# Expert rows gathered as quarters and turned by VectorE's block transposes

## The chip, the cores and the metric

The kernel runs on one core of a Trainium2 chip. The metric is device time in microseconds, of one launch. The core has TensorE (PE: matmuls and their weight loads), VectorE (DVE), ScalarE (ACT), GpSimd (POOL, which also issues the indirect transfers here) and SyncE (SP, which issues the others), and 16 DMA engines that all transfers share.

## What is computed

A residual block for 2048 tokens of 1024 features in float32: a token mixer (gated linear attention and sliding-window attention), then a mixture of 32 experts with two experts a token, then a final norm. The change lies in the experts:

```python
def hier_moe(u, ...):                      # u = rms_norm(h) * norm2_w
    g_w, g_idx = top_k(softmax(hf @ w_group + b_group), 1)        # one group of 4
    e_val, e_idx = top_k(logits of the 8 experts of the group, 2)
    gate = softmax(e_val) * g_w
    # rows sorted by expert; for every expert e and its rows xb:
    y = (silu(xb @ w_gate[e]) * (xb @ w_up[e])) @ w_down[e]       # 1024 -> 512 -> 1024
    out[token] += gate * y
h = h + hier_moe(rms_norm(h, norm2_w)); y = rms_norm(h, final_norm_w)
```

## The kernel before

**Stages.** The mixer runs first, 128 tokens an iteration, some 935 us. It leaves the residual rows in HBM (scratch "h", the trace's h_dram) and the normalised rows, without the weight norm2, in scratch "v2" (v_dram). Routing follows (`routing`), until about 970 us: every token-expert pair gets a slot, and tables of indices are made. Then comes the loop over the 32 experts (`experts`), 971.7 to 1759.3 us, and a short end. An expert has 160 slots: 128 main rows and 32 in a "tail". What exceeds them goes to a path for overflow, which the functions named `..._over` hold and which has no work in these runs. By the number of its rows an expert is computed 128, 144 or 160 wide (`WIDTHS`, `by_width`).

**How the parts talk.** Each engine runs its own loop over the experts, and semaphores hold them together. `after(eng, "m_", name, n)` waits until n steps of `name` are done in all.

**One expert on TensorE** (`pe_chunk`): `pe_gate` (L1324), four groups of eight matmuls into G = banks 0 and 1; `pe_up` (L1337), the same into U = banks 2 and 3; `pe_x` for the next expert, steps 0 and 1: eight transposes (L1291) of the gathered rows by a matmul with the identity, into banks 4 and 5; the down product of the tail into bank 0 (L1351, not at width 128); the first half of the down product of the main rows into bank 6 (L1365); `pe_x` step 2, two transposes of the tail's quarters; at 144 and 160 the matmul L1372, which sums the tail's squares over its four quarters and waits for ScalarE's `m_tail_square`; the second half of the down product into bank 7. The next gate waits for the tail's sum, since both use bank 0.

**VectorE:** four products `hT` = U x silu(G) (L1433); `dve_x` for the next expert, which evacuates the transposed rows times norm2 into `xT` (L1409, L1414); `dve_tail` (L1441), which adds the tail's rows, held as quarters of 256 columns on four groups of 32 partitions, to `sums_quarters`, once the base rows have landed; `dve_sums` (L1449, two halves); `dve_scale` (L1457, L1458), which makes the output rows from the roots.

**ScalarE:** four SiLUs (L1379), the tail's squares (L1389), the main rows' squares (L1392).

**POOL** (an iteration e): `copy_index` (L1277) once the transposes of expert e+1 are done, `gather` for expert e+2, as one transfer of 128 rows of 4 KB (L1264) and one of 128 quarter rows of 1 KB for the tail (L1266), into `xg`; then `move`: the move indices (L1199), `put_sums` (L1212, L1214: the sums of expert e to h_dram), `roots` (L1220, L1222), and, when the put has landed, `gather_base` (L1204, L1206: base rows of expert e+1 from h_dram, to which its result is added), and `put_out` (L1227, L1229). The base rows can only be gathered after the sums of the last expert have landed, since a token has two experts. Before the loop the rows of experts 0 and 1 are gathered.

**SyncE:** w_gate, w_up and w_down of the next expert (2 MB each, L1189), each as soon as its last matmul of this one is done. There is one buffer of each.

## Time and profile before

| | us |
|---|---|
| median of three runs | 1778.04 (1775.43 to 1778.35) |
| the profiled execution, as a whole | 1777.08 |
| its span, first to last instruction | 1774.8 |
| TensorE busy in the span | 1710.6 (96%) |
| VectorE, ScalarE, POOL busy | 669.0, 503.7, 387.6 |
| first gate to the last expert's end on TensorE | 971.7 to 1759.3 |

All durations below come from the profiled execution. The time of an execution is its span and some 2 us around it. A busy TensorE is not a TensorE at its peak, since ends of matmuls are modelled: what a group of matmuls costs is read from start to start.

### The profile page before, as it was taken

How to read it: one execution, taken by the hardware profiler on the slowest of the kernel's cores; microseconds unless marked ns; L12 is line 12 of the kernel's file. 1: busy time of each engine (PE TensorE's matmuls, PEld its weight loads, DVE VectorE, ACT ScalarE, POOL GpSimd, SP SyncE). 2: the span in 40 equal slices, each digit the busy share in tenths (PEclk: the TensorE clock that was granted, in tenths of full speed). 3: DMA queues.
4: the chain of work that ended last, by engine and by line, in shares of the span. 5: the costliest groups of instructions: out<-in, count | busy, mean ns of one | idle time of the engine just before them, and what ended most of it. 6: DMA issues, size and time to landing. Idle time of an engine off the chain costs nothing. (4 is left out here: it accounts for less than half of the span.)

```text
span 1774.8 us, 31842 instructions
## 1 busy us (share of the span) xinstructions
PE 1710.6 (96%) x11222; PEld 1271.9 (72%) x11223; DVE 669.0 (38%) x1721; ACT 503.7 (28%) x1318; POOL 387.6 (22%) x522
## 2 busy tenths in 40 slices
PE   6899999999999999999968999999999999999996
PEld 5676675766757667676647788778878788878784
DVE  1344345543455434554357222222222222222222
ACT  1444424444244442444423111111111111111111
POOL 0001011010100101001011234334434344434333
PEclk9999999999999999999989999999999999999998
DMA  9521122211222112121124889889999999989994
GB/s 356 119 74 47 60 83 71 71 47 59 83 71 71 45 61 83 71 71 43 63 93 151 299 293 353 309 308 329 325 332 340 301 339 330 339 306 350 324 313 138
DMA packets 156873, 333.69 MB, mean 188 GB/s; under 512 B 23797, under 2 KB 43482, under 8 KB 156836
## 3 DMA queue, kind: packets, MB, share of 16 engines
q1 hardware_dynamic: 131204, 277.82, 46.0%
q0 software_dynamic: 24768, 55.26, 8.8%
q8 instruction: 25, 0.41, 0.1%
q10 hardware_dynamic: 864, 0.10, 0.0%
q14 instruction: 12, 0.10, 0.0%
HBM read 298.74 MB, written 63.70 MB: 204 GB/s over the span
## 5 line engine op out<-in xcount | busy, mean ns | idle before, releaser
L328 PE MATMUL bank<-uT,w_in_sb 128*128 128x128 f32 x2304 | 277.2, 279 | 2.3 <-DVE uT L676 2.3
L328 PEld LDWEIGHTS bank<-uT,w_in_sb 128*128 128x128 f32 x2304 | 268.3, 195 | 11.1 <-issue 8.9
L1324 PEld LDWEIGHTS bank<-xT,wts 128*128 128x128 f32 x2048 | 248.6, 191 | 29.9 <-issue 22.8
L1324 PE MATMUL bank<-xT,wts 128*128 128x128 f32 (+2 forms) x2048 | 253.9, 283 | 9.5 <-DVE sums L1449 4.5
L322 PE MATMUL bank<-w_in_sb,uT 128*128 128x512 f32 (+1 forms) x768 | 261.5, 494 | 0.0
L1337 PE MATMUL bank<-xT,wts 128*128 128x128 f32 (+2 forms) x2048 | 247.9, 282 | 0.0
L1337 PEld LDWEIGHTS bank<-xT,wts 128*128 128x128 f32 x2048 | 245.0, 191 | 0.0
L1365 PE MATMUL bank<-wts,hT 128*128 128x512 f32 x512 | 232.9, 597 | 0.0
L350 PE MATMUL bank<-w_out_sb,mixT 128*128 128x512 f32 x512 | 222.7, 593 | 1.5 <-ACT mixT L550 0.8
L322 PEld LDWEIGHTS bank<-w_in_sb,uT 128*128 128x128 f32 x768 | 127.1, 190 | 110.2 <-issue 110.2
L872 POOL TENSOR_SCALAR ss<-ss 128x1 f32<-128x1 f32 (+1 forms) x49 | 9.4, 192 | 803.0 <-ACT junk L600 432.6
L350 PEld LDWEIGHTS bank<-w_out_sb,mixT 128*128 128x128 f32 x512 | 96.0, 190 | 116.5 <-issue 114.3
L1365 PEld LDWEIGHTS bank<-wts,hT 128*128 128x128 f32 x512 | 92.2, 190 | 97.6 <-issue 97.6
L1433 DVE TENSOR_TENSOR hT<-bank,sg 128x160 f32<-128x160 f32 x128 | 41.5, 325 | 251.4 <-PE bank L1337 251.4
L1389 ACT ACTIVATE squares<-sums_quarters 128x256 bf16<-128x256 f32 x32 | 13.3, 417 | 371.5 <-DVE sums_quarters L1441 371.5
L1457 DVE SCALAR_TENSOR_TENSOR rows<-sums,means,fw 128x1024 f32<-128x1024 f32 x32 | 41.1, 1285 | 145.1 <-issue 125.0
L1204 POOL DMA_INDIRECT sums<-h_dram,movec x32 | 35.8, 1118 | 196.3 <-DMA h_dram<-sums_quarters,movec 195.4
L1392 ACT ACTIVATE squares<-sums 128x1024 bf16<-128x1024 f32 x32 | 33.8, 1057 | 152.2 <-DVE sums L1449 152.2
L1449 DVE SCALAR_TENSOR_TENSOR sums<-bank,gatec,sums 128x512 f32<-128x512 f32 x64 | 47.7, 746 | 67.4 <-PE bank L1365 67.3
L1379 ACT ACTIVATE sg<-bank 128x160 f32<-128x160 f32 x128 | 38.9, 304 | 116.8 <-PE bank L1324 114.9
L610 ACT ACTIVATE sc<-sc,sm 128x192 f32<-128x192 f32 x128 | 56.3, 441 | 50.5 <-DVE sm L861 50.5
L1291 PEld LDWEIGHTS bank<-ident,xg 128*128 128x128 f32 x330 | 39.4, 141 | 17.5 <-issue 17.5
(261 smaller groups left out, 1836.8 us busy)
## 6 DMA issues: line engine op xcount, KB each, us to landing
wts<-w_gate_in SPq DMA_DIRECT2D x32, 2048.0 KB, 10.0
wts<-w_up_in SPq DMA_DIRECT2D x32, 2048.0 KB, 10.5
wts<-w_down_in SPq DMA_DIRECT2D x32, 2048.0 KB, 11.0
x_sb<-x_in SPq DMA_DIRECT2D x17, 512.0 KB, 3.9
xT_in<-x_t_in SPq DMA_DIRECT2D x17, 512.0 KB, 4.8
w_in_sb<-w_in_in SPq DMA_DIRECT2D x4, 2048.0 KB, 12.0
h_sb<-x_in SPq DMA_DIRECT2D x16, 512.0 KB, 3.3
h_dram<-h_sb SPq DMA_DIRECT2D x16, 512.0 KB, 2.6
```

The source lines that it names most:

```text
L322: m = pe.matmul(bk[name][:, col:col + hi - lo], uT[:, k, :], w_in[:, k, lo:hi], start=k == 0, stop=k == KD - 1)
L328: m = pe.matmul(bk[name][0:hi - lo, col:col + P], w_in[:, k, lo:hi], uT[:, k, :], start=k == 0, stop=k == KD - 1)
L350: m = pe.matmul(bk[f"wo{n}"][:, :], mixT[:, k, :], w_out[:, k, n * 512:(n + 1) * 512], start=k == HA, stop=k == HA - 1)
L610: act.activation(sc[:, hh, :], sc[:, hh, :], ACT.Exp, bias=nm[:, hh:hh + 1], accum_out=sums[:, hh:hh + 1])
L1291: m = pe.transpose(XB[j % 2][:, c * P:(c + 1) * P], src, ident)
L1324: m = pe.matmul(G[m_ % 2][:, 0:w], wg[:, k, m_ * P:(m_ + 1) * P], xT[:, k, 0:w], start=k == 0, stop=k == KD - 1)
L1337: m = pe.matmul(U[m_ % 2][:, 0:w], wu[:, k, m_ * P:(m_ + 1) * P], xT[:, k, 0:w], start=k == 0, stop=k == KD - 1)
L1365: m = pe.matmul(YB[half][:, :], hT[:, k, 0:P], wd[:, k, half * 512:(half + 1) * 512], start=k == 0, stop=k == KF - 1)
L1379: act.activation(sg[:, m_, 0:n_], G[m_ % 2][:, 0:n_], ACT.Silu).then_inc(sem(pre + "sg_ready"), 1)
L1433: nc.vector.tensor_tensor(hT[:, m_, 0:n_], U[m_ % 2][:, 0:n_], sg[:, m_, 0:n_], ALU.mult)\
L1449: nc.vector.scalar_tensor_tensor(base[:, cols], YB[half][:, :], gatec[:, 0:1], base[:, cols], ALU.mult, ALU.add)\
L1457: nc.vector.scalar_tensor_tensor(rows[:, :], base[:, :], mean[:, 2:3], K["fw"][:, :], ALU.mult, ALU.mult).then_inc(sem("scaled"), 1)
```

## The change

The mixer is as it was. In the experts:

- **Gathers.** All 160 slots of an expert are gathered in five pieces (`gather`, PIECES = 5) of 32 slots. A piece is an indirect transfer of 128 quarter rows of 1 KB: partition 32q + j gets quarter q of the row of slot j. The bytes are as before. The indices come from a table `idxq` (five columns an expert), which routing makes with five small matmuls in place of one.
- **Turning.** VectorE turns `xg` in blocks of 32x32 into `xT` (`dve_x`: two transposes of 128x640) and multiplies it in place with `norm2q` (two products). Feature 256q + 32k + i then lies on partition 32q + i of k-step k. The host lays w_gate and w_up out to match. TensorE's transposes are gone, and with them `pe_x`.
- **Order on TensorE.** Three k-steps of the first down half now stand ahead of the tail's product, the fourth behind it.
- **Order on VectorE.** All of `dve_x` stands ahead of `dve_tail`.
- **Order on POOL.** Pieces 0 to 2 ahead of `move`, pieces 3 and 4 after the roots (when the first gate group of the next expert is done), before the base gather. Before the loop, expert 0 is gathered, and expert 1 after the first base rows. For the last expert the outputs are put before the sums.
- The gather for expert n waits until VectorE has turned expert n-1 (`m_xg_taken`); the rows of two experts are in one buffer, one after the other, as before.

```diff
+    def gather(po, pieces=range(PIECES)):
+        for t in pieces:
+            po.indirect_dma_start(out=xq[:, t * CAP:(t + 1) * CAP], in_=quarters(scratch["v2"]), out_offset=None,
+                                  in_offset=bass.IndirectOffsetOnAxis(ap=idxm[:, t:t + 1], axis=0)).then_inc(sem("m_xg_loaded"), 16)
+
     def move(po, n, last=False):
 
+        if not last:
+            copy_pieces(po, n + 2)
+            gather(po, range(3))
         wait_apart(po, idx_rider, (sem("base_loaded"), 32 * n + 32), (sem("rows_put"), 32 * n))
         rows_of(po, 6 * n + 6)
         wait_apart(po, idx_rider, (sem("move_index_ready"), n + 2))
+        if last:
+            roots(po, n)
+            put_out(po, n)
+            put_sums(po, n)
+            return
         put_sums(po, n)
         roots(po, n)
-        if not last:
-            wait_apart(po, idx_rider, (sem("sums_put"), 32 * n + 32), (sem("scaled"), 2 * n + 2))
-            gather_base(po)
+        wait_apart(po, idx_rider, (sem("m_g_done"), 4 * n + 5 + CREDIT))
+        gather(po, range(3, PIECES))
+        wait_apart(po, idx_rider, (sem("sums_put"), 32 * n + 32), (sem("scaled"), 2 * n + 2))
+        gather_base(po)
         put_out(po, n)
...
+    def dve_x(v_, n):
+
+        wait(v_, sem("m_xg_loaded"), 16 * PIECES * (n + 1))
+        after(v_, "m_", "u_done", 4 * n)
+        for half in range(2):
+            ks = slice(4 * half, 4 * half + 4)
+            nc.vector.transpose(xT[:, ks, 0:MAIN].rearrange("p k (t j) -> p t k j", j=TAIL),
+                                xq.rearrange("p (t k i) -> p t k i", t=PIECES, k=KD)[:, :, ks, :]).then_inc(sem("m_xg_turned"), 1)
+            wait(v_, sem("m_xg_turned"), 2 * n + half + 1)
+            m = nc.vector.tensor_tensor(xT[:, ks, 0:MAIN], xT[:, ks, 0:MAIN], norm2q[:, ks].unsqueeze(2).to_broadcast([P, 4, MAIN]), ALU.mult)
+            m.then_inc(sem("m_xT_ready"), 1)
+        v_.sem_inc(sem("m_xg_taken"), 1)
...
             with v_.Fori(0, NE) as e:
                 dve_h(v_, "m_", e)
-                dve_x(v_, e + 1, range(2))
+                dve_x(v_, e + 1)
                 dve_tail(v_, e)
-                dve_x(v_, e + 1, range(2, 3))
                 dve_sums(v_, e)
                 dve_scale(v_, e)
```

TensorE, the end of an expert 144 wide, before (bank 6 and 7 are the two halves of the down product, bank 0 the tail's):

```order
L1291 MATMUL bank4<-ident,xg 128x128 x4
L1291 MATMUL bank5<-ident,xg 128x128 x4
...
L1351 MATMUL bank0<-wts,hT 32x256 x16
...
L1365 MATMUL bank6<-wts,hT 128x512 x4
...
L1291 MATMUL bank4<-ident,xg 128x128 x2
...
L1372 MATMUL bank2<-quarter_means,quad 128x2
...
L1365 MATMUL bank7<-wts,hT 128x512 x4
```

and the same place now:

```order
L1351 MATMUL bank6<-wts,hT 128x512 x3
...
L1368 MATMUL bank0<-wts,hT 32x256 x16
L1351 MATMUL bank6<-wts,hT 128x512
...
L1375 MATMUL bank2<-quarter_means,quad 128x2
...
L1351 MATMUL bank7<-wts,hT 128x512 x4
```

The transposes are gone, the tail's product has moved behind three k-steps of bank 6, and the small matmul on bank 2 stands right behind the fourth.

VectorE, the same expert after its last hT, before (xT is written for the next expert):

```order
L1409 TENSOR_TENSOR xT<-bank4,norm2_sb 128x4x128
...
L1409 TENSOR_TENSOR xT<-bank5,norm2_sb 128x4x128
...
L1441 SCALAR_TENSOR_TENSOR sums_quarters<-bank0,gatec,sums_quarters 128x256
...
L1414 TENSOR_TENSOR xT<-bank4,norm2_sb 128x4x32 x2
...
L1449 SCALAR_TENSOR_TENSOR sums<-bank6,gatec,sums 128x512
```

and now:

```order
L1428 STREAM_TRANSPOSE xT<-xg 128x5x4x32
...
L1431 TENSOR_TENSOR xT<-xT,norm2q 128x4x160
L1428 STREAM_TRANSPOSE xT<-xg 128x5x4x32
...
L1431 TENSOR_TENSOR xT<-xT,norm2q 128x4x160
...
L1458 SCALAR_TENSOR_TENSOR sums_quarters<-bank0,gatec,sums_quarters 128x256
...
L1466 SCALAR_TENSOR_TENSOR sums<-bank6,gatec,sums 128x512
```

Four instructions on SBUF stand where two evacuations of banks stood, and the last evacuation behind the tail's sum has moved ahead of it.

POOL, an iteration of the loop, before (xg are gathers of rows, h_dram the sums put, sums the base rows):

```order
L1277 COPY idxc<-idx 128x2
...
L1264 DMA xg<-v_dram,idxc 128x1024
L1266 DMA xg<-v_dram,idxc 128x256
...
L1199 COPY movec<-moves 128x6
...
L1212 DMA h_dram<-sums,movec 2304x1024
L1214 DMA h_dram<-sums_quarters,movec 9216x256
...
L1222 TENSOR_TENSOR means<-means,power 128x2
...
L1204 DMA sums<-h_dram,movec 128x1024
```

and now:

```order
L1246 COPY idxm<-idxq 128x5
...
L1252 DMA xg<-v_dram,idxm 128x256 x3
...
L1206 COPY movec<-moves 128x6
...
L1219 DMA h_dram<-sums,movec 2304x1024
L1221 DMA h_dram<-sums_quarters,movec 9216x256
...
L1229 TENSOR_TENSOR means<-means,power 128x2
...
L1252 DMA xg<-v_dram,idxm 128x256 x2
...
L1211 DMA sums<-h_dram,movec 128x1024
```

Three of the five pieces take the place of the two gathers, and two have come in between the roots and the base gather.

## Rows read from the trace of the kernel before

**Rows 1.** Busy time by engine, TensorE's clock, DMA share and GB/s, 1200 to 1700
```profile
1200.00:1700.00 500.00, 499.01 (x3478) 409.66 (x3477) 136.55 (x287) 88.75 (x208) 195.58 (x250) 1.00 0.95 329
```
**Rows 2.** Groups by line and shape, 971.72 to 1759.3, gate at width 128
```profile
L1324 PE MATMUL bank<-xT,wts 128*128 128x128 f32 x1152 | 136.5, 277 | 4.8 <-issue 2.8 <-DVE xT L1414 0.9
```
**Rows 3.** Timeline (start, duration, instruction, idle before), TensorE, widths 128 and 144
```profile
1200.22 7.64 PE L1324 MATMUL bank<-xT,wts 128*128 128x128 f32 x64
...
1214.85 1.04 PE L1291 MATMUL bank<-ident,xg 128*128 128x128 f32 x8
...
1215.72 3.60 PE L1365 MATMUL bank<-wts,hT 128*128 128x512 f32 x8
...
1222.81 8.07 PE L1324 MATMUL bank<-xT,wts 128*128 128x144 f32 x64
...
1238.56 1.04 PE L1291 MATMUL bank<-ident,xg 128*128 128x128 f32 x8
1239.53 1.93 PE L1351 MATMUL bank<-wts,hT 128*32 128x256 f32 x32
1241.39 3.70 PE L1365 MATMUL bank<-wts,hT 128*128 128x512 f32 x8
1244.93 0.38 PE L1291 MATMUL bank<-ident,xg 128*128 128x128 f32 x2
1245.15 0.28 PE L1372 MATMUL bank<-quarter_means,quad 128*128 128x2 f32 x2
...
1248.81 7.64 PE L1324 MATMUL bank<-xT,wts 128*128 128x128 f32 x64
```
**Rows 4.** Timeline, VectorE and ScalarE, the expert of width 144
```profile
1238.82 0.32 DVE L1433 TENSOR_TENSOR hT<-bank,sg 128x160 f32<-128x160 f32 x1 [1.64 <-PE bank L1337]
...
1243.36 0.48 DVE L1441 SCALAR_TENSOR_TENSOR sums_quarters<-bank,gatec,sums_quarters 128x256 f32<-128x256 f32 x1 [2.66 <-DMA sums_quarters<-h_dram,movec]
1243.88 0.42 ACT L1389 ACTIVATE squares<-sums_quarters 128x256 bf16<-128x256 f32 x1 [12.48 <-DVE sums_quarters L1441]
1244.20 0.19 ACT L1389 ACTIVATION_READ_ACCUMULATOR squares<-sums_quarters 128x1 f32 x1
```
**Rows 5.** Timeline, POOL, from the index copy to the base gather
```profile
1219.79 0.18 POOL L1277 COPY idxc<-idx 128x2 int32 x1 [1.35 <-PE bank L1291]
1220.80 1.01 POOL L1264 DMA_INDIRECT xg<-v_dram,idxc  x1 [0.83 <-POOL idxc L1277]
...
1223.88 0.19 POOL L1199 COPY movec<-moves 128x6 int32 x1 [0.79 <-DMA out<-rows_quarters,movec]
...
1225.12 1.01 POOL L1212 DMA_INDIRECT h_dram<-sums,movec  x1 [1.05 <-issue]
...
1235.43 1.11 POOL L1204 DMA_INDIRECT sums<-h_dram,movec  x1 [6.89 <-DMA h_dram<-sums_quarters,movec]
```
**Rows 6.** Landing of the sums' puts (L1212), 1000 to 1740
```profile
DMA to landing us min/median/max: 6.6/7.5/9.0
```
**Rows 7.** Groups by shape, whole span: a block transpose and products on VectorE
```profile
L705 DVE TENSOR_TENSOR sc<-sc,sm 128x1024 f32<-128x1024 f32 x16 | 19.5, 1218 | 0.0
L726 DVE STREAM_TRANSPOSE u2T<-u2T 128x1024 f32<-128x1024 f32 x15 | 18.5, 1233 | 0.0
...
L705 DVE TENSOR_TENSOR g_t<-sc,sm 128x512 f32<-128x512 f32 x16 | 11.1, 692 | 0.6
```
**Rows 8.** DMA issues: weights of the up product, KB each, us to landing
```profile
wts<-w_up_in SPq DMA_DIRECT2D x32, 2048.0 KB, 10.5
```
**Rows 9.** Timeline, first gather, first gate and last issue
```profile
961.36 1.23 POOL L1264 DMA_INDIRECT xg<-v_dram,idxc  x1 [0.96 <-POOL idxc L1277]
...
971.72 7.66 PE L1324 MATMUL bank<-xT,wts 128*128 128x128 f32 x64 [0.88 <-DVE xT L1414]
...
1768.53 0.99 POOL L1229 DMA_INDIRECT out<-rows_quarters,movec  x1 [0.30 <-issue]
```
**Rows 10.** Timeline, VectorE beside the first gather
```profile
960.80 2.31 DVE L1111 TENSOR_TENSOR column<-column,gates 128x456 f32<-128x456 f32 x4
```

More of the change, by code:

```diff
@@ L52 @@
 TAIL = 32
+PIECES = MAIN // TAIL
 SPARE = 2 * P
@@ L1040, in pe_part @@
         pe.wait_ge(sem("spread_args"), 1)
-        pe.matmul(bank[3][:, 0:NE], rep[:, 0:P], idx_f[:, :], start=True, stop=True).then_inc(sem("slot_sums"), 1)
+        for t in range(PIECES):
+            m = pe.matmul(bank[3][:, t * NE:(t + 1) * NE], rep[:, t % 4 * P:(t % 4 + 1) * P], idx_f[:, t // 4, :], start=True, stop=True)
+        m.then_inc(sem("slot_sums"), 1)
         keep_clock(pe, 3)
@@ L1300, in pe_x_over @@
             for kk in range(2):
-                c = slice((2 * j + kk) * P, (2 * j + kk + 1) * P)
                 for part in range(2):
-                    m = pe.transpose(XB[j % 2][:, kk * CAP + part * P:kk * CAP + (part + 1) * P], xg[:, part, c], ident)
+                    for a in range(4):
+                        m = pe.matmul(XB[j % 2][a * TAIL:(a + 1) * TAIL, kk * CAP + part * P:kk * CAP + (part + 1) * P],
+                                         xg[:, part, a * CAP + (2 * j + kk) * TAIL:a * CAP + (2 * j + kk + 1) * TAIL], ident,
+                                      start=True, stop=True)
             m.then_inc(sem(pre + "x_done"), 1)
@@ L1338, in pe_up, with pe_down, pe_chunk @@
             m.then_inc(sem(pre + "u_done"), 1)
-    def pe_chunk(pe, pre, n, w, next_x):
-        pe_gate(pe, pre, n, w)
-        pe_up(pe, pre, n, w)
-        next_x((0, 1))
-        wait(pe, sem(f"{pre}w_down_loaded"), 16 * (n + 1))
-        after(pe, pre, "h_ready", 4 * n + 4)
-        if P < w <= MAIN:
+    def pe_down(pe, bank_, n, half, rows, ks):
+        for k in ks:
+            m = pe.matmul(bank_[:, :], hT[:, k, rows], wd[:, k, half * 512:(half + 1) * 512], start=k == 0, stop=k == KF - 1,
+                          skip_group_check=True)
+        return m
+    def pe_chunk(pe, n, w):
+        main = slice(0, P)
+        pe_gate(pe, "m_", n, w)
+        pe_up(pe, "m_", n, w)
+        wait(pe, sem("m_w_down_loaded"), 16 * (n + 1))
+        after(pe, "m_", "summed", 3 * n - 1)
+        after(pe, "m_", "h_ready", 4 * n + 3)
+        pe_down(pe, YB[0], n, 0, main, range(KF - 1))
+        after(pe, "m_", "h_ready", 4 * n + 4)
+        if w > P:
             for k in range(KF):
@@ L1663, in _ @@
             rt_pe(pe)
-            pe_x(pe, 0, range(3))
             rt_pe_last(pe)
@@ L1726, in _ @@
             po.sem_inc(sem("o_y_free"), CREDIT)
-            for e in range(2):
-                copy_index(po, "m_", e, 2 * e)
-                gather(po)
+            copy_pieces(po, 0)
+            gather(po)
             po.wait_ge(sem("spare_cleared"), 16 * SPARE // P)
```

160 lines of the change are left out of this document (70 added, 90 removed).

## The prediction

> **What bounds the kernel now.** I read the windows of busy time first: between 1200 and 1700 us TensorE is busy for 499.0 of 500 us at the full granted clock, while the DMA engines show a share of 0.95 at 329 GB/s [rows 1]. So the expert stage is bound by TensorE's instruction stream, with DMA close behind. The groups by shape then give the population: 1152 gate matmuls of width 128 at 64 instructions an expert are 18 experts of width 128; the other 14 are 144 or 160 wide [rows 2]. The timeline of TensorE gives the anatomy [rows 3]. An expert of width 128 has 14.63 us of gate and up (1200.22 to 1214.85), then 7.96 us until the next gate (to 1222.81), 22.59 in all. One of width 144 has 15.75 and 10.25 us. I call the end of the up group U (1214.85, 1238.56) and count from it. The small TensorE transposes L1291 lie in the stream itself: they hold it for 0.97 + 0.22 us in the wide case, 0.87 + 0.22 in the narrow one (the second pair is the same in both). They also cover the wait for the last hT, which VectorE ends at U + 0.58 [rows 4].
>
> Off that stream runs a loop through HBM: POOL puts sums (L1212, I call its start P), waits for the landing, gathers the next base rows (L1204), and VectorE's tail sum (L1441) waits for them. In the expert shown, 10.31 us from P to the gather (1225.12 to 1235.43) and 7.93 from there to the tail sum at 1243.36, which ended on that DMA [rows 4, 5]. The two together are 18.2 us. The put's own landing runs 6.6 to 9.0 us, median 7.5 [rows 6], so I take 17.2 as the mean of the loop (an estimate from these rows) and 16 to 19.5 as its spread. Before, this is just hidden: P is at U + 10.27 (1225.12), the rows land at 10.3 + 17.2 = 27.5, and the next U of a narrow expert is at 22.6, so at U + 4.9 of the next, against a next gate at U + 7.96.
>
> **The change, part by part.** *TensorE's transposes go:* 18 x 1.09 + 14 x 1.19 = 36.3 us off the stream. The cover for hT is replaced: the first three k-steps of the first down group run for 3/4 of 3.54 us (1241.39 to 1244.93), 2.66 us, against a wait of 0.6. That costs nothing.
>
> *VectorE turns the rows:* two transposes of 128x640 and two multiplications with both inputs in SBUF. The trace has a transpose of 1024 elements at 1233 ns, and products of 1024 and 512 at 1218 and 692 ns [rows 7]. By the slope of the latter pair 640 elements are 0.82 us; the transpose less the same slope is 0.84. Four of them with short waits on their own semaphore are 3.5 us, from U + 0.6 to U + 4.1. The first half of xT is thus ready at U + 2.3, against the next gate at U + 6.87. Hidden, if the five pieces have landed.
>
> *The tail sum now stands behind those 3.5 us, and a matmul behind the tail sum.* In the wide case TensorE does 2.66 (three k-steps) + 1.86 (tail, 1239.53 to 1241.39) = U + 4.5; the tail sum starts at 4.8. Then ScalarE's squares follow 0.5 us after it and take 0.42 and the accumulator's read, so the matmul L1372 can go 1.1 us after the tail sum starts, U + 5.9. TensorE has done its last k-step (0.88) at U + 5.4. So 0.5 us wait, 14 x 0.5 = 7 us. Before, L1372 stood behind another 3.54 us at U + 6.59 and did not wait [rows 3]. Late base rows now stop it directly. After a narrow expert they land 27.3 after its U (below), and the wide U is 6.87 + 15.75 = 22.6 later: U + 4.7 on average, up to U + 7.0. On average another 0.25 us: 3.5 us.
>
> *POOL:* an expert's gathers are 5 issues for 2. An issue lasts about 1.0 us whatever it moves, plus 0.3 of gap. Three stand ahead of the put: the index copy at U + 4.3, its first issue 1.01 later as now (1219.79 to 1220.80), the two issues with their gap 2.29, a third 1.3, so the copy of the move index at U + 8.9, and the put 1.24 after it (1223.88 to 1225.12) at P = U + 10.1 [rows 5]. That is where it is now, though the sums are ready a microsecond earlier: POOL's order, not TensorE, sets P for narrow experts. The other two issues stand between roots and base gather, in time in which POOL waits for the put's landing; they end about P + 6.6 against 10.3, and cost nothing. Base rows then land at 10.1 + 17.2 = 27.3, while the next narrow U comes at 6.87 + 14.63 = 21.5: U + 5.8, with a range from 4.6 to 8.1. The gate needs the tail sum (0.5) and some 0.4 until it starts: U + 6.7 against 6.87. No wait at the mean, 2.1 us at the worst; I take 0.15 on average, 18 x 0.15 = 2.7 us. This is the thinnest cover of the whole sum.
>
> *The bytes* are the same. The weights have room: up rows land in 10.5 us [rows 8] and are needed after a down and a gate group, some 14.3 us.
>
> *The start:* five issues from about 961.8 (961.36 now, plus 0.4 for four more small matmuls) end their landing near 970, VectorE turns until 973.6, the gate that started at 971.72 [rows 9] is held up in its first group, and SiLU waits for constants that VectorE writes behind it: +2.7 us. *The end:* after the last expert the outputs are put before the sums; the outputs leave 1.0 us earlier, but two more issues of 1.3 follow. The last one stands at 1768.53 now [rows 9]; this costs 1.5 us.
>
> **Sum:** -36.3 + 7 + 3.5 + 2.7 + 2.7 + 1.5 = -18.9 us. The profiled execution took 1777.08 us in all (span 1774.8), 1 us under the median of the three. 1777.1 - 18.9 = 1758.2, so **1758 us**.
>
> [...]
>
> **Rivals.** (1) *The put-and-gather loop gets slower and becomes the bound* (the slower side). Place: L1441 waits for base rows, behind it L1372 and the next gate. For it: DMA share is already 0.95, everything is to run 3% denser, and two gathers now queue between put and base gather. Against it: no weight load is late, and fewer bytes stand ahead of the put. Working: with the loop at L, a chain over two narrow experts is 14.63 + 10.1 + L + 0.9 from a gate to the one after the next; at L = 19.2 that is 44.8, 22.4 an expert, so nearly all of 1.09 is gone; wide experts lose the same through L1372. Each microsecond beyond the mean therefore costs some 15 us over 32 experts; +1.25 us breaks even (1777). At +2 us, with the wide experts now waiting 2 us each, it is about 1795.
>
> (2) *VectorE's two products hold up POOL.* In narrow experts POOL issues the outputs at U + 1.8 to 4.1, beside VectorE's 1.64 us of two-input products. A full lock delays P by up to 1.6 us, and by the price above, on the narrow experts alone, leaves about 1770. What the trace has: at 960.80 VectorE ran such products for 2.31 us, and the POOL issue that began at 961.36 amid them took 1.23 us instead of 1.01 [rows 9, 10, 5]. That is 0.2, not a lock.
>
> (3) *The cover is better than I think*: the matmul L1372 hardly waits and landings shrink since the series ahead of the put is shorter. Then -36.3 + 2.7 + 1.5 = -32: 1745.
>
> (4) *The change moves nothing*: the stream is not what sets the pace, since the DMA engines are full, and TensorE's freed time turns into waits for weights. At 0.95 share there is 5% left, and the narrow expert wants 4.8% of it. It would show as gate or up waiting for wts; then 1774 to 1780.
>
> **How the numbers follow.** Forecast, between 1750 and 1768: 0.57. Rival 3: 0.08. Rival 2, about 1770: 0.13. Rival 4 with a half-strength rival 1, within 0.2% of before (1774.5 to 1781.6, about what a measurement of this kernel can tell): 0.08. Rival 1: 0.14. Faster 0.78, same 0.08, slower 0.14. The range goes from 1745, the floor of the costs, to 1782, where the loop is 1.5 us longer; it leaves out the worse part of rival 1.
>
> **What would show it.** Distance from gate to gate near 21.5 us for narrow experts (22.59 now) and 25.3 for 144 wide (26.00 now). VectorE's transpose at 0.84 and product at 0.82 us, all four inside 3.6. L1372 waiting 0.5 to 1 us for ScalarE's squares in each wide expert. P at U + 10.1, first gate at 974. Wrong, if P to L1204 exceeds 11.5 us, if the gate waits for the tail sum in more than a few narrow experts, if VectorE waits for the row pieces, or if TensorE waits for wts.

## The result, and the profile after

| | before | changed |
|---|---|---|
| median, us | 1776.97 (1775.43 to 1778.35, 4 runs) | 1746.20 (1745.01 to 1747.92, 4 runs) |
| span of the profiled execution, us | 1774.8 | 1746.0 |
| TensorE, VectorE, POOL busy, us | 1710.6, 669.0, 387.6 | 1679.8, 719.6, 528.8 |

The ratio of the times is 0.9828, with a 95% interval of 0.9811 to 0.9845: 30.8 us less, where 18.9 were forecast. The profiled executions differ by 28.8 us of span; the account below is made of those. The changed kernel's is the slowest of its four, so 2 us lie between the two ways of counting.

The window of [rows 1] in the changed kernel (busy time of TensorE, weight loads, VectorE, ScalarE, POOL, then clock, DMA share, GB/s):

```profile
1200.00:1700.00 500.00, 496.03 (x3379) 398.56 (x3378) 173.67 (x299) 89.26 (x210) 293.24 (x319) 1.00 0.96 339
```

TensorE is still the bound, at the same full clock; the DMA engines went from 329 to 339 GB/s, so they had room for it. VectorE has 37 us more work in this window and POOL 98 more.

TensorE on the two experts of [rows 3], 128 and 144 wide (start, duration, instruction, idle before):

```profile
1190.30 7.64 PE L1333 MATMUL bank<-xT,wts 128*128 128x128 f32 x64
1197.78 7.31 PE L1346 MATMUL bank<-xT,wts 128*128 128x128 f32 x64
1204.92 7.03 PE L1351 MATMUL bank<-wts,hT 128*128 128x512 f32 x16
1211.79 8.07 PE L1333 MATMUL bank<-xT,wts 128*128 128x144 f32 x64
1219.70 8.00 PE L1346 MATMUL bank<-xT,wts 128*128 128x144 f32 x64
1227.54 2.74 PE L1351 MATMUL bank<-wts,hT 128*128 128x512 f32 x6
1230.21 1.93 PE L1368 MATMUL bank<-wts,hT 128*32 128x256 f32 x32
1232.08 1.13 PE L1351 MATMUL bank<-wts,hT 128*128 128x512 f32 x2
1233.29 0.38 PE L1375 MATMUL bank<-quarter_means,quad 128*128 128x2 f32 x2
1233.54 3.68 PE L1351 MATMUL bank<-wts,hT 128*128 128x512 f32 x8
1237.05 6.19 PE L1333 MATMUL bank<-xT,wts 128*128 128x128 f32 x51
```

From gate to gate the narrow expert takes 21.49 us (22.59 before) and the wide one 25.26 (26.00). The narrow one got its whole 1.09. The wide one got 0.74 of 1.19: from the last k-step (1232.08) to the second half (1233.54) are 1.46 us, for 0.88 of k-step and 0.14 of L1375, and the missing 0.44 is L1375's wait.

VectorE there (the last product of one expert, then the turning of the rows for the next), and below it the groups over 1000 to 1700 (instructions, then busy time and mean ns, then idle time before them and what ended it):

```profile
1205.18 0.33 DVE L1450 TENSOR_TENSOR hT<-bank,sg 128x160 f32<-128x160 f32 x1 [1.46 <-PE bank L1346]
1205.52 0.84 DVE L1428 STREAM_TRANSPOSE xT<-xg 128x640 f32<-128x640 f32 x1
1206.40 0.83 DVE L1431 TENSOR_TENSOR xT<-xT,norm2q 128x640 f32<-128x640 f32 x1
...
1209.41 0.48 DVE L1458 SCALAR_TENSOR_TENSOR sums_quarters<-bank,gatec,sums_quarters 128x256 f32<-128x256 f32 x1 [0.57 <-DMA sums_quarters<-h_dram,movec]
...
1228.98 0.84 DVE L1428 STREAM_TRANSPOSE xT<-xg 128x640 f32<-128x640 f32 x1 [0.85 <-DMA xg<-v_dram,idxm]
```
```profile
L1428 DVE STREAM_TRANSPOSE xT<-xg 128x640 f32<-128x640 f32 x59 | 49.6, 841 | 15.6 <-DMA xg<-v_dram,idxm 15.2 <-issue 0.2
L1431 DVE TENSOR_TENSOR xT<-xT,norm2q 128x640 f32<-128x640 f32 x58 | 47.9, 825 | 2.0
...
L1458 DVE SCALAR_TENSOR_TENSOR sums_quarters<-bank,gatec,sums_quarters 128x256 f32<-128x256 f32 x29 | 14.0, 482 | 14.5 <-DMA sums_quarters<-h_dram,movec 8.0 <-PE bank L1368 6.4
```

841 and 825 ns were forecast as 0.84 and 0.82. What was not: VectorE waits for the row pieces, 15.2 us in this window, up to 2 us at a time.

POOL, and what VectorE ran beside it:

```profile
1195.67 1.28 DVE L1474 SCALAR_TENSOR_TENSOR rows<-sums,means,fw 128x1024 f32<-128x1024 f32 x1 [4.36 <-issue]
1195.78 2.11 POOL L1252 DMA_INDIRECT xg<-v_dram,idxm  x1 [0.20 <-issue]
...
1196.88 0.48 DVE L1475 SCALAR_TENSOR_TENSOR rows_quarters<-sums_quarters,means,fw_quarters 128x256 f32<-128x256 f32 x1
...
1198.20 0.97 POOL L1252 DMA_INDIRECT xg<-v_dram,idxm  x1 [0.30 <-issue]
```
```profile
1208.02 0.83 DVE L1431 TENSOR_TENSOR xT<-xT,norm2q 128x640 f32<-128x640 f32 x1
1208.29 0.60 POOL L1246 COPY idxm<-idxq 128x5 int32 x1 [1.71 <-DVEq L1433]
...
1215.47 1.01 POOL L1219 DMA_INDIRECT h_dram<-sums,movec  x1 [1.06 <-issue]
...
1224.39 1.02 POOL L1211 DMA_INDIRECT sums<-h_dram,movec  x1 [1.91 <-issue]
```

The put starts at U + 10.5 (1215.47 against 1204.92), the base gather 8.92 us behind it, where [rows 5] had 10.31. The first of the two pieces takes 2.11 us, the other 0.97. The difference, 1.14, is what was left of VectorE's product when the issue began (1195.67 + 1.28 - 1195.78 = 1.17). The index copy that begins amid L1431 takes 0.60 us, for 0.20 where it stands alone. From put to base gather the mean over experts 2 to 30 is 8.46 us here and 9.75 in the kernel before.

The start and the end, for [rows 9]:

```profile
973.24 10.35 PE L1333 MATMUL bank<-xT,wts 128*128 128x128 f32 x64 [2.09 <-DVE xT L1431]
...
999.45 7.65 PE L1333 MATMUL bank<-xT,wts 128*128 128x128 f32 x64 [1.84 <-DVE sums L1466]
```
```profile
1739.91 0.97 POOL L1221 DMA_INDIRECT h_dram<-sums_quarters,movec  x1 [0.30 <-DMA out<-rows_quarters,movec]
```

The first gate group takes 10.19 us from start to start, for 7.50 before. For most of it the granted clock is 0.50 of full speed, 1.2 GHz (the window of 6.8 us, columns as above):

```profile
972.60:979.40 6.80, 6.16 (x29) 6.16 (x30) 3.96 (x13) 1.59 (x2) 1.40 (x3) 0.50 0.16 65
```

TensorE had stood for 2.09 us ahead of it. The ten other kernels with the new experts, all at the full clock there, take 9.18 to 9.20 us for this group, so 1.0 of its 2.7 us more is the clock.

### The profile page after: what moved, and what is told of

It is laid out like the page before. It is cut to its first block, busy times and chain, and to the rows that moved or that the text cites. A ratio compares the mean times of both kernels' runs of the same rounds, so it can differ in the third digit from the quotient of the medians.

```text
span 1746.0 us, 31293 instructions
## 1 busy us (share of the span) xinstructions
PE 1679.8 (96%) x10900; PEld 1236.8 (71%) x10901; DVE 719.6 (41%) x1721; ACT 503.7 (29%) x1318; POOL 528.8 (30%) x621
## 4 chain that ended last, share of the span: by engine, by line
PE 81%; DMA 5%; issue 5%; DVE 4%; ACT 3%; POOL 2%; ACTq 0%; POOLq 0%; DVEq 0%
PE bank L329 15%; PE bank L323 15%; PE bank L351 12%; PE bank L1346 11%; PE bank L1351 9%; PE bank L1333 9%; DMA xg<-v_dram,idxm 2%; PE bank L318 2%; DMA h_dram<-sums_quarters,movec 2%; PE bank L501 1%; PE bank L1368 1%; POOL xg L1252 1%; PE bank L408 1%; ACT L1397 1%; PE bank L450 1%
## 5 line engine op out<-in xcount | busy, mean ns | idle before, releaser
L1252 POOL DMA_INDIRECT xg<-v_dram,idxm x165 | 196.5, 1191 | 65.4 <-issue 31.0
L1474 DVE SCALAR_TENSOR_TENSOR rows<-sums,means,fw 128x1024 f32<-128x1024 f32 x32 | 41.1, 1285 | 167.4 <-issue 154.3
L1428 DVE STREAM_TRANSPOSE xT<-xg 128x640 f32<-128x640 f32 x66 | 55.5, 841 | 18.8 <-DMA xg<-v_dram,idxm 18.4
## 6 DMA issues: line engine op xcount, KB each, us to landing
w_in_sb<-w_in_in SPq DMA_DIRECT2D x4, 2048.0 KB, 12.1
```

The lines of the kernel that those rows point to most:

```text
L1252: po.indirect_dma_start(out=xq[:, t * CAP:(t + 1) * CAP], in_=quarters(scratch["v2"]), out_offset=None, in_offset=bass.IndirectOffsetOnAxi ...
L1428: nc.vector.transpose(xT[:, ks, 0:MAIN].rearrange("p k (t j) -> p t k j", j=TAIL), xq.rearrange("p (t k i) -> p t k i", t=PIECES, k=KD)[:, ...
```

## The experiments

Each kernel was timed beside the kernel before on the same chip. Ratios are to it, with 95% intervals, and spans are of one profiled execution each. 0.001 of the ratio is 1.8 us. Except where a heading says otherwise, the edit is made to the changed kernel, whose span is 1746.0.

### Are TensorE's transposes the gain? The ten put back

```diff
         pe_up(pe, "m_", n, w)
+        for c in range(10):
+            pe.transpose(XB[c // 4 % 2][:, c % 4 * P:(c % 4 + 1) * P], ident, ident)
```

> The changed kernel with ten TensorE transposes of the identity put back into the stream of every expert, behind the up product, into two banks that nothing reads. Theory (the gain is the stream's length): each costs what it cost before, 0.11 us, less the covered waits: 18 x 1.09 + 14 x 1.19 = 36 us minus some 6 us of waits for the squares in wide experts, that move apart: +28 to +36, 1774 to 1782. Rival (the DMA engines or the loop bound the kernel, TensorE has slack now): under +15 us.

Measured: 1782.19 us (1777.71 to 1788.61), ratio 1.0018 (1.0000 to 1.0036), span 1776.5. The whole gain is gone, though VectorE and POOL still work the new way. TensorE, a narrow expert:

```profile
1205.79 7.31 PE L1346 MATMUL bank<-xT,wts 128*128 128x128 f32 x64
1212.93 1.25 PE L1361 MATMUL bank<-ident 128*128 128x128 f32 x10
1214.03 7.03 PE L1351 MATMUL bank<-wts,hT 128*128 128x512 f32 x16
```

The ten hold the stream for 1.10 us, and the expert is back at 22.59. The theory stands. By the ratios 34 us came back, by the spans 30.5. The stream of 32 experts alone is 35 us longer; of what the spans lack, 2.7 us are waits for late rows that it covers again, and the rest lies in the start and the first three experts.

### The kernel before with seven of ten transposes left out

```diff
-            for c in range(4 if j < 2 else 2):
+            for c in range(1):
```

> The kernel before with one transpose of 128x128 for each of TensorE's three steps that turn an expert's rows, in place of four, four and two: seven of ten left out, so that seven tenths of the rows that the experts work on are wrong. Nothing else differs. Theory (the transposes lie in the bounding stream, 0.87 and 0.22 us a narrow expert, 0.97 and 0.22 a wide one): 7 x 0.109 = 0.76 us an expert, -24 us, span near 1751, narrow experts at 21.8 us. Rival (the stream isn't what sets the pace, since the DMA engines are 95% busy): under 5 us, narrow experts stay above 22.4.

Measured: 1766.12 us (1765.70 to 1766.83), ratio 0.9924 (0.9898 to 0.9949), span 1764.5. That is 10.3 us less than before by the spans and 13.5 by the ratio (9 to 18), where 24 were expected. The narrow expert went from 22.59 to 22.42 and not to 21.8. Both sides missed the time; the rival's "above 22.4" came true without its reason, that TensorE's stream does not set the pace. TensorE behind the up group:

```profile
1259.19 0.38 PE L1291 MATMUL bank<-ident,xg 128*128 128x128 f32 x2
1259.90 3.69 PE L1365 MATMUL bank<-wts,hT 128*128 128x512 f32 x8 [0.33 <-DVE hT L1433]
1263.43 0.27 PE L1291 MATMUL bank<-ident,xg 128*128 128x128 f32 x1
```

Two transposes end 0.22 us after U, the down product needs the last hT, and it starts at U + 0.71. In [rows 3] the eight ran until U + 0.87, so 0.71 of these 0.87 us was cover that something else must give. Taking the transposes out alone, in the old order, would have left most of their price where it was. The gain of the change is that of two edits.

### The other edit alone: the tail's product first again

Three k-steps of the first down half need only the first three hT. Here they go back behind the tail's product, so that the down products begin with one that needs all four.

```diff
-        after(pe, "m_", "h_ready", 4 * n + 3)
-        pe_down(pe, YB[0], n, 0, main, range(KF - 1))
         after(pe, "m_", "h_ready", 4 * n + 4)
...
-        pe_down(pe, YB[0], n, 0, main, range(KF - 1, KF)).then_inc(sem("m_d_done"), 2 if w == P else 1)
+        pe_down(pe, YB[0], n, 0, main, range(KF)).then_inc(sem("m_d_done"), 2 if w == P else 1)
```

> The changed kernel with TensorE's order undone: TensorE waits for the fourth hT before any down product, and the tail's product stands ahead of all four k-steps of the first half. Theory (the three k-steps cover a wait of 0.6 us that the transposes covered before): narrow experts +0.6 us each, 18 x 0.6 = 11 us; wide ones +0.6 at the start, less 0.4 since L1375 then finds the squares ready, 14 x 0.2 = 3; together +14, 1760. Rival (the order does not matter, a matmul group hides that latency anyway): 1746.

Measured: 1758.65 us (1757.22 to 1759.78), ratio 0.9890 (0.9865 to 0.9915), span 1755.4, so 9.4 us more. TensorE's groups over 1000 to 1700:

```profile
L1351 PE MATMUL bank<-wts,hT 128*128 128x512 f32 x464 | 209.8, 601 | 7.6 <-DVE hT L1448 7.6
...
L1366 PE MATMUL bank<-wts,hT 128*32 128x256 f32 x416 | 25.1, 382 | 6.1 <-DVE hT L1448 6.1
```

0.47 us of idle time in front of every down product, 13.7 in the window. The narrow expert takes 22.23 us (+0.73). The wide one takes 25.44 (+0.18) only: in this order L1375 no longer waits and gives back its 0.44. The theory had counted both, 18 x 0.6 + 14 x 0.2 = 14 us; measured are 18 x 0.73 + 14 x 0.18 = 15.7. The span grew by less since the longer stream covers the late rows (2.6 us) and since the start and the third gate group came out 3.8 us shorter, of which 1.0 is the clock of the first gate group.

### L1375's wait

The small matmul moves behind three k-steps of the second down half.

```diff
+        after(pe, "m_", "summed", 3 * n)
+        pe_down(pe, YB[1], n, 1, main, range(KF - 1))
         if w > P:
             after(pe, "m_", "tail_square", n + 1)
...
-        after(pe, "m_", "summed", 3 * n)
-        pe_down(pe, YB[1], n, 1, main, range(KF)).then_inc(sem("m_d_done"), 1)
+        pe_down(pe, YB[1], n, 1, main, range(KF - 1, KF)).then_inc(sem("m_d_done"), 1)
```

> The changed kernel with one matmul moved: L1375, which sums the tail's squares over the quarters and waits for ScalarE, stands ahead of the last k-step of the second down half instead of ahead of the first. Theory (TensorE's stream sets the pace, and this wait is the only part of my sum that the change pays in every wide expert): the 14 wide experts lose their wait, 0.45 us each, and the five intervals with late base rows lose some 0.6 us each, so -7 to -9 us against the changed kernel, about 1738. Rival (the loop of put and base gather through HBM sets the pace by now): the wait turns up again as a gate waiting for the tail's sum, no gain, 1746.

Measured: 1741.33 us (1739.81 to 1742.12, 5 runs), ratio 0.9791 (0.9769 to 0.9812), span 1738.0. TensorE, the wide expert:

```profile
1230.20 3.70 PE L1351 MATMUL bank<-wts,hT 128*128 128x512 f32 x8
1233.74 0.28 PE L1377 MATMUL bank<-quarter_means,quad 128*128 128x2 f32 x2
1233.88 1.10 PE L1351 MATMUL bank<-wts,hT 128*128 128x512 f32 x2
```

No wait is left, and the wide expert takes 24.90 us for 25.26. Fourteen times 0.36 is 5.0 of the 8.0 us. Another 2.5 are the four experts that had waited 0.55 to 0.87 us for a late tail sum (13, 19, 20 and 27, counted from 0), which lost all but 0.13 of it. The last 0.4 is the balance of the start: the first gate came 0.98 us sooner and its group kept the full clock (1.0), but the second gate group ran for 3.4 us at the granted clock 0.50 (1.2 GHz), after TensorE had stood for 1.84 us, and took 8.87 us for 7.49. The loop did not take the gain.

### Does POOL's order set the time? All pieces ahead of the put

```diff
             copy_pieces(po, n + 2)
-            gather(po, range(3))
+            gather(po)
...
-        wait_apart(po, idx_rider, (sem("m_g_done"), 4 * n + 5 + CREDIT))
-        gather(po, range(3, PIECES))
```

> The changed kernel with the POOL order undone: all five pieces ahead of the put, none between roots and base gather. Theory (the split is what keeps the loop under TensorE's stream): the put starts 2.6 us later in narrow experts, at U + 12.7, base rows land at about U + 8.4 of the next, gate and tail sum wait: 17 x 1.0 + 14 x 0.6, so +20 to +25 us, 1766 to 1771. Rival (POOL's order is covered anyway, the gain is only TensorE's transposes): within 3 us of 1746, since the base gather then has nothing ahead of it and starts earlier after the put.

Measured: 1751.39 us (1748.99 to 1754.16), ratio 0.9852 (0.9824 to 0.9879), span 1747.2. The theory fell: 1.2 us of span, 4 by the ratio, for 20 to 25. The rival had said within 3 us. VectorE over 1000 to 1700:

```profile
L1426 DVE STREAM_TRANSPOSE xT<-xg 128x640 f32<-128x640 f32 x58 | 48.8, 841 | 0.5
...
L1456 DVE SCALAR_TENSOR_TENSOR sums_quarters<-bank,gatec,sums_quarters 128x256 f32<-128x256 f32 x29 | 14.0, 484 | 28.9 <-DMA sums_quarters<-h_dram,movec 19.1 <-PE bank L1366 9.7
```

The put did start later, at U + 12.1 on average over experts 2 to 30 (11.0 in the changed kernel). But base rows also came sooner after it: from the put to a tail sum that the landing released are 16.0 us on average (13 cases), 17.5 in the changed kernel (10 cases; not the same experts). Only 0.3 us of that lies ahead of the base gather (8.18 us behind the put, for 8.46). The rest lies behind it, where no transfer of pieces has been issued just ahead of the base rows; that this is the reason is argued, not shown. And the wait for row pieces fell from 15.2 us to nothing. In narrow experts the put came 1.7 us later (U + 12.2 for 10.5), not 2.6, and the rest of the loop was wrongly held fixed.

### The pieces held back by 1.4 us

This one was made to see the 2.11 us: pieces 3 and 4 also wait until VectorE has scaled the rows.

```diff
-        wait_apart(po, idx_rider, (sem("m_g_done"), 4 * n + 5 + CREDIT))
+        wait_apart(po, idx_rider, (sem("m_g_done"), 4 * n + 5 + CREDIT), (sem("scaled"), 2 * n + 2))
```

> The changed kernel with pieces 3 and 4 waiting also until VectorE has scaled the output rows, so that no piece starts beside VectorE's product of two SBUF inputs of 1.28 us. Theory (that product holds up the issue that starts beside it: 2.11 us for 0.96): every third piece takes 0.95 to 1.0 us, and the time doesn't move, since POOL then waits for the put's landing anyway: span 1745 to 1748. Rival for the duration (the third piece is long of itself, the first issue behind the roots): it stays at 2.1 us, and the two end 1 us later.

Measured: 1773.85 us (1766.00 to 1780.28, 10 runs), ratio 0.9962 (0.9939 to 0.9986), span 1766.3. POOL's issues, and VectorE over 1000 to 1700:

```profile
1203.44 1.06 POOL L1252 DMA_INDIRECT xg<-v_dram,idxm  x1 [2.63 <-PE bank L1333]
1204.81 0.97 POOL L1252 DMA_INDIRECT xg<-v_dram,idxm  x1 [0.30 <-issue]
```
```profile
L1428 DVE STREAM_TRANSPOSE xT<-xg 128x640 f32<-128x640 f32 x58 | 48.8, 842 | 31.1 <-DMA xg<-v_dram,idxm 24.9 <-issue 6.0
```

On the duration the theory holds: 1.06 us for 2.11 once the product is over. On the time it is far off. The last piece's issue now ends 10.3 us after the gate (1205.78 against 1195.51), 8.9 in the changed kernel (1199.17 against 1190.30), and these 1.4 us cost 20.3 of span, 24 by the ratio. VectorE's wait for pieces went from 15.2 to 24.9 us, everything behind it on VectorE came late, and TensorE with it. The base gather moved as well, but only by 0.4 us from the put (8.86 for 8.46). In two stretches of 3.4 us, after long stalls, TensorE ran at the granted clock 0.50, which costs 3.4 of the 20.3 us. The landing of the pieces has no slack to speak of. It is a second loop beside the one through h_dram, and the forecast had put it at no cost.

### Doses on the loop from put to base rows

Two, three and five idle roots of 0.72 us on POOL between the put's landing and the base gather.

```diff
         wait_apart(po, idx_rider, (sem("sums_put"), 32 * n + 32), (sem("scaled"), 2 * n + 2))
+        for j in range(2):
+            nc.gpsimd.tensor_tensor(K["pad"][:, 2 * j:2 * j + 2], K["pad"][:, 12:14], K["power"][:, 0:2], ALU.pow)
         gather_base(po)
```

> The changed kernel with two idle roots (of 128x2 each, written to a tile that nobody reads) on POOL between the landing of the put and the gather of the base rows. The trace has one root at 0.72 us, so the loop from put to base rows is some 1.5 us longer. Theory (that of the first rival's price: the loop has about 1.2 us of slack and each further microsecond costs some 15 us over the experts): by the price on record +4 us; worked out afresh from the changed kernel's trace, where a wide expert behind a narrow one has no slack (tail sum at U + 4.7 with rows landed at the same time) and a narrow one behind a narrow one about 1.0: 9 x 1.5 + 8 x 0.5 = +17 us, so a span near 1763 and a ratio near 0.992 to before. Other theory, from the run in which the put started 1.2 us later and cost 1.2 us in all: the landing of the rows isn't what sets the pace; then +0 to +3 us, span 1746 to 1749.

> The same with five idle roots, some 3.7 us more in the loop from put to base rows. Theory, from slacks of 0 (wide behind narrow, 9), 1.0 (narrow behind narrow, 8) and 2.0 us (behind a wide one, 13, of which the wide ones have more): 9 x 3.7 + 8 x 2.7 + 7 x 1.7 = +67 us, span near 1813, ratio about 1.02; by the price on record, 15 us for each microsecond beyond 1.2, +37 us, span 1783, ratio 1.003. The tail sum waits for the DMA in nearly every expert behind a narrow one. Other theory, the loop isn't what sets the pace: under +10 us, span below 1756, and the distance between gates stays at 21.5 for narrow experts.

> The changed kernel with three idle roots in the loop, 2.2 us; two cost nothing (span 1745.2 for 1746.0), five cost 42.7 us. With two, the gather was issued 0.85 us later on average and the rows came 0.8 us sooner behind it. Theory (the wait behind the gather is elastic by about 1 us and then gives nothing more; 15 us for each microsecond that is left): the gather is 1.5 us later, 0.5 to 0.7 of it is left over, +7 to +12 us, span 1753 to 1758. Rival (a threshold: what is left under 2 us of delay is covered, and the five roots were past a cliff): under +3 us, span below 1749. A straight line from zero would give +25 us.

| roots | put to base gather, mean | put to a tail sum released by the landing, mean (cases) | span | median |
|---|---|---|---|---|
| 0 | 8.46 | 17.47 (10) | 1746.0 | 1746.20 |
| 2 | 9.30 | 17.54 (14) | 1745.2 | 1745.53 |
| 3 | 10.21 | 18.18 (14) | 1755.1 | 1758.27 |
| 5 | 11.41 | 20.26 (15) | 1788.7 | 1793.56 |

The ratios are 0.9812 (0.9783 to 0.9840), 0.9880 (0.9847 to 0.9914) and 1.0090 (1.0059 to 1.0121). The two middle columns are means over experts 2 to 30. VectorE's tail sum in 1000 to 1700, with two, three and five:

```profile
L1460 DVE SCALAR_TENSOR_TENSOR sums_quarters<-bank,gatec,sums_quarters 128x256 f32<-128x256 f32 x29 | 14.0, 483 | 19.8 <-DMA sums_quarters<-h_dram,movec 12.2 <-PE bank L1370 7.6
```
```profile
L1460 DVE SCALAR_TENSOR_TENSOR sums_quarters<-bank,gatec,sums_quarters 128x256 f32<-128x256 f32 x29 | 14.0, 484 | 32.3 <-DMA sums_quarters<-h_dram,movec 22.3 <-PE bank L1370 7.3 <-PE bank L1353 2.5
```
```profile
L1460 DVE SCALAR_TENSOR_TENSOR sums_quarters<-bank,gatec,sums_quarters 128x256 f32<-128x256 f32 x28 | 13.5, 483 | 65.1 <-DMA sums_quarters<-h_dram,movec 56.8 <-PE bank L1370 8.3
```

Two roots cost nothing: the gather goes out 0.84 us later and its rows come 0.8 us sooner behind it. Against the loop as it came out, and not against the dose, +0.71 us cost 9.1 us of span and +2.79 cost 42.7, so 13 and 15 us for each microsecond. The loop is a mean over those experts alone whose tail sum waited for the landing, and these are not the same in each run, so the price is an estimate. With five roots it also holds the clock: six stretches at 0.50 of full speed, 24 us in all, of which TensorE was busy for 22, so up to 11 of the 42.7 us. With three roots there is none. The prediction's price of 15 holds roughly; the theory worked out afresh, which took every root for loop time, gave 17 and 67 and missed both.

### The same dose on the kernel before

> The kernel before with the same five idle roots (some 3.6 us) between the landing of the put and the gather of the base rows. In the changed kernel they cost 42.7 us. Theory (the change used up slack that the loop had before): rows landed at 4.8 after U against a need at 7.1 in a narrow expert behind a narrow one, and at 3.6 against 5.5 in a wide one behind a narrow one, so 8 x 1.2 + 9 x 1.7 = +25 us here, span near 1800, at least 10 us less than in the changed kernel. Other theory (the loop was as tight before): +40 us or more, span 1815 and up.

Measured: 1816.94 us (1812.38 to 1827.58), ratio 1.0201 (1.0164 to 1.0239): 36 us more than before, 29 to 43 by the interval. In the changed kernel the same roots cost 2.6% of the ratio, 47 us, 40 to 53 with both intervals. The profiled execution is the slowest of its four (span 1825.7) and is not used for this. By the medians the changed kernel is 11 us more sensitive, as the theory said, but the absolute 36 is nearer to the other theory's 40 than to 25, and the two intervals overlap. Part of the 11 us is the clock: its mean over an execution lies at 0.987 to 0.990 without roots and at 0.982 to 0.986 with them here, and at 0.988 to 0.989 and 0.980 to 0.984 in the changed kernel. That the change used up slack in this loop is not settled. VectorE's wait for base rows was not shorter before:

```profile
L1441 DVE SCALAR_TENSOR_TENSOR sums_quarters<-bank,gatec,sums_quarters 128x256 f32<-128x256 f32 x28 | 13.5, 484 | 59.2 <-DMA sums_quarters<-h_dram,movec 27.9 <-PE bank L1365 26.2 <-PE bank L1351 5.0
```

27.9 us in the kernel before without roots, 8.0 after: what was idle time in front of the tail sum is now filled with the turning of rows.

### The second gate, and both remedies together

```diff
             gather(po)
+            copy_pieces(po, 1)
+            gather(po)
...
             first_base(po)
-            copy_pieces(po, 1)
-            gather(po)
```

> The changed kernel with expert 1's five pieces gathered straight behind expert 0's, ahead of the first base rows. Theory: VectorE's wait for these pieces before it turns them goes (2.60 us), and with it the second gate's 1.84 us: -1.5 to -2.5 us, span near 1744. Rival: the base rows now land later by the five issues (6 us), and the tail sum of expert 0 waits for them instead: 0 to +3 us, the first distance between gates 26.2 or more.

Measured: 1745.11 us (1742.82 to 1749.43, 5 runs), ratio 0.9812 (0.9788 to 0.9835), span 1743.8, 2.2 us less. The times of the two kernels overlap, so only the rows decide, and they decide against the theory's mechanism:

```profile
988.76 7.03 PE L1351 MATMUL bank<-wts,hT 128*128 128x512 f32 x16
997.56 2.72 PE L1333 MATMUL bank<-xT,wts 128*128 128x128 f32 x22 [1.76 <-DVE sums L1466]
```

VectorE no longer waits for expert 1's pieces (it turns them from 989.64), yet the second gate still stands 1.76 us. The first gate group kept the full clock here and took 9.18 us for 10.19; that is 1.0 of the 1.09 us by which the first distance is shorter (25.12 for 26.21), and the edit did not make it. VectorE's sum, which the row names, is not what these gates wait for: in a plain narrow expert of the kernel before the next gate starts ahead of that sum's end, at U + 7.96 against 8.91. The kernel before has such gaps too, 2.84 us ahead of its second gate, and these two, ahead of the third and the seventh (gates are counted from 1):

```profile
1021.87 2.30 PE L1324 MATMUL bank<-xT,wts 128*128 128x160 f32 x15 [1.78 <-DVE sums L1449]
```
```profile
1118.93 3.25 PE L1324 MATMUL bank<-xT,wts 128*128 128x160 f32 x22 [1.41 <-DVE sums L1449]
```

The DMA traffic has a candidate. A queue named "instruction" moves single packets of 16 KB; in the kernel before it has six of them between 1050 and 1700, in the changed kernel none:

```profile
q8 instruction: 6, 0.10, 0.1%
```

Of these one ends 1.61 us ahead of the seventh gate and one 3.33 ahead of the ninth, and an earlier one ends 1.59 ahead of the third. The other four show no gap of more than 0.1 us. In all 14 traces the second gate starts 3.1 to 3.2 us behind the end of such a packet, whatever was edited, and in the kernels with all pieces ahead of the put, with the start swapped and with three transposes left a gap inside the third gate group ends 1.5 to 1.6 us behind one (with the transposes put back, one ahead of the third gate, 1.9 behind). So these gaps look like waits for the program's own instructions, and neither for rows nor for sums. That is a match of times in kept traces; no run was made for it, and the trace does not say for which engine a packet is.

> Both remedies together: the matmul over the tail's squares stands ahead of the last k-step of the second down half (in all 14 wide experts), and expert 1's pieces are gathered before the first base rows. Theory, the two are independent: the first is worth 8.0 us by its own run, the second 1.5 to 2.5 us (the second gate waited 1.84 us for the sums of expert 0 behind VectorE's wait of 2.60 for the pieces of expert 1), so a span of 1735.5 to 1736.5 and a ratio near 0.978. Rival: with the pieces ahead, the first base rows land later and expert 0's tail sum waits for them instead, so nothing beyond the first remedy: span 1738, ratio 0.979.

Measured: 1740.33 us (1738.10 to 1742.33, 5 runs), ratio 0.9782 (0.9760 to 0.9804), span 1736.5. This is the fastest of all; that it is faster than the one with L1375 moved alone (1741.33, ratio 0.9791) can't be told at these intervals. Against the changed kernel they are 7 and 8 us faster by the ratios, 8.0 and 9.5 by the spans.

## Why the prediction was right in direction, and short by a third

The table sets each term of the sum against the profiled executions. It counts by distances from gate to gate: 764.98 us over 31 of them before (971.72 to 1736.70), 735.20 after (973.24 to 1708.44). Experts are counted from 0. A stall is what a distance has beyond the plain one of its width (22.59, 26.00 and 27.63 before, 21.50, 25.26 and 26.90 after).

| term | forecast | measured |
|---|---|---|
| transposes off TensorE | -36.3 | -36.3 (1.09 and 1.19 an expert) |
| L1375's wait, 14 times | +7 | +6.3 (0.45 each) |
| late rows, wide and narrow | +6.2 | +2.1 |
| start, to the second gate | +2.7 | +3.2 |
| gaps ahead of the gates 3, 7 and 9 (gates counted from 1) | - | -4.5 |
| end, and the rest | +1.5 | +0.4 |
| sum | -18.9 | -28.8 |

**What held.** *TensorE's stream is the bound, and the transposes lie in it.* Narrow experts at 21.50 (forecast 21.5), wide at 25.26 (25.3); putting the transposes back gave all of it back. *VectorE's four instructions* take 841 and 825 ns, and fit into 3.6 us. *L1375* waited 0.45 us in a wide expert for ScalarE's squares, for 0.5, and the kernel that moves it got 0.36 of it back. *The start*: the first gate came at 973.24, for 974, and its group waited for xT and for ScalarE as said (9.18 us for 7.50 at the full clock). That the whole term fits, 3.2 for 2.7, is luck: 1.5 of a later gate, 1.7 of these waits and 1.0 of a lower clock, less 1.0 by which the gap ahead of the second gate is shorter. *The loop*: 17.5 us (10 cases) where 17.2 was taken, but the kernel before has 18.2 (11 cases), so the loop became shorter and the forecast had taken it for equal. A microsecond of it costs 13 to 15 us, for 15. The gain would be gone at some 1.9 us more of loop, by a line between the doses; 1.25 was said, for a smaller gain. *Weights*: no gate or up group waited for wts, so the fourth rival, that the full DMA engines would not let the stream go faster, fell with 339 GB/s.

**The steps that were off** are two terms of about equal weight. One is the late rows: "On average another 0.25 us: 3.5 us" for the wide experts and "I take 0.15 on average, 18 x 0.15 = 2.7 us" for the narrow ones. The changed kernel has 2.7 us of them in all, 0.68 at expert 13, 0.55 at 19, 0.57 at 20 and 0.87 at 27, and the kernel before had 0.55 of the same (0.33 and 0.22 at 26 and 27), which belongs off the sum. The mean of the loop was near and its spread too wide: between 1000 and 1700 the landing of the base rows released 10 of 29 tail sums, and only that of expert 19 too late. The other term was left out: the kernel before has 5.0 us of gaps ahead of the gates 3, 7 and 9 (1.95, 1.57 and 1.46), the changed one 0.5, inside its third gate group. [Rows 9] end with the first gate, and the sum took the rest of the stream for plain. All of them end 1.5 to 3.3 us behind a packet of the instruction queue, of which the changed kernel has none after 1050 us. So the 4.5 us are, by this match of times, code that arrives late in the kernel before and not the work of the experts. Whether every execution of the kernel before has these packets, and why the changed kernel has not, is open; how much of the 4.5 us is chance can't be told from one profiled execution of each.

**A mechanism put aside that is there.** The second rival was put at 0.13 with the words "That is 0.2, not a lock". It is a lock, in one direction: a POOL instruction that begins amid a VectorE product of two SBUF inputs takes longer by what is left of the product, or a little less. Beside L1474 an issue takes 2.11 us for 0.97, in 31 of the 31 experts that have it. Beside L1431, where it was expected, the index copy takes 0.60 us for 0.20, also 31 times, and ends with the product; the one issue of outputs that begins there takes 1.23 us for 1.00. The copy stands ahead of the put, the issue of 2.11 us behind it; whether the copy's 0.4 us moved the put no run shows. [Rows 10] is one row for four short products, and POOL's issue began 0.01 us after the second of them did; it was 0.2 longer. In the kernel with all pieces ahead of the put two issues that begin 0.02 and 0.03 us into L1429, the same product there, are not longer at all, and six that begin later are, by 0.2 to 0.6. The Trainium skill, page "SBUF — State Buffer", section "SBUF: two separate sides", states that a VectorE instruction with two SBUF inputs locks the shared ports only against a GpSimd operation that reads SBUF, and that whichever of the two starts first has them for its whole instruction while the other fully blocks. The first part agrees: the copy and the issues beside L1474 read their indices from SBUF. The second agrees for POOL behind VectorE alone. L1475, with two SBUF inputs, begins amid such an issue 31 times and takes 0.48 us, as it does alone (1196.88 above), and L1431 begins amid an issue of outputs four times and takes 0.83. So here an issue does not hold up a product.

**"They end about P + 6.6 against 10.3, and cost nothing"** was true for the base gather and missed the other end. The two pieces themselves must land before VectorE turns the rows, at U + 0.6. "Hidden, if the five pieces have landed" was said, and not worked out. They had not: behind the start VectorE waited for them in 15 experts, 0.2 to 2.1 us each, which is one of the four signs of being wrong that the prediction names, and three of the four stalls named above (13, 20, 27) stand behind late turning and not behind late base rows. Holding the pieces back by 1.4 us showed the price, 20 us. The lock adds 1.1 us just there.

**The third rival**, cover better than thought, at 1745 and with 0.08, came out nearest in time. Half of its reason did too: from put to base gather, which waits for the put's landing, are 8.46 us on average for 9.75 before. The other half did not, since L1375 waits as forecast.

**What stays open:** whether late instructions hold the single gates that stand for 1.4 to 2.8 us, which only the match of times says; why the changed kernel has fewer of these packets; and whether the loop was as tight before.

## What to carry to other kernels

A filler in the bounding stream may be the cover of a wait: seven tenths of these transposes taken out alone gave 10 us (13.5 by the ratio), and with three k-steps moved in front of the wait ten tenths gave 29. Before a stall is added to a sum, list the stalls of the old kernel, distance by distance, and take off what it has of the same. Look for the clock in each stretch before a longer group is put down to a wait. When a transfer is moved to where its queue is idle, ask not only what it delays there but when its own bytes are wanted.

## What the runs showed that was not expected

- *A POOL issue begun beside a VectorE product of two SBUF inputs* waits for it: 2.11 us for 0.97 beside a product of 1.28 us, and 1.06 when it starts after. A product that begins amid an issue is not held up. This is how the lock looks in a trace: one row of a series is longer by the rest of the neighbour's row.
- *Landings are elastic.* With the base gather sent 0.84 us later the tail sums that waited for it began at the same time; sent 1.75 us later they began 0.71 us later, sent 2.95 us later, 2.79. Transfers that share 16 engines at a share of 0.96 with 2 MB weight loads don't land at issue plus a constant.
- *Loops a microsecond short are steep.* One microsecond of landing time costs 13 to 15 us over the 32 experts, here in either loop. A part of it is the clock: in the execution with five roots the granted clock fell to 0.50 six times, for 24 us in all.
- *A gate group can wait for instructions*, as far as times tell: gaps that the view puts down to "issue" or to a VectorE sum long done end 1.5 to 1.9 or 3.1 to 3.3 us behind a 16 KB packet of the queue "instruction".
